# Two hybrid decoder layers in one core: the mean of each post-norm as two fp32r products of the sum's high and low part, placed one triple further on

## What is computed

```
def rmsnorm(x, g):
    xf = x.astype(jnp.float32)
    y = xf * lax.rsqrt(jnp.mean(xf * xf, axis=-1, keepdims=True) + RMS_EPS)
    return (y * g.astype(jnp.float32)).astype(x.dtype)
...
        x = x + rmsnorm(y, norm_post[i])
        gate = jax.nn.sigmoid(rmsnorm(x, pe_norm[i]) @ pe_w_gate[i])
        x = x + gate * (p[i] @ pe_w_proj[i])
```

## Time and profile before

| what | value |
| --- | --- |
| median of three executions | 636.34 us (635.78 to 637.64) |
| the profiled execution | 636.59 us |
| its span, first to last instruction | 634.5 us |
| granted TensorE clock, mean | 1.000 |
| PE busy | 625.3 us (99%) |
| weight loads on PE | 516.1 us (81%) |
| DVE busy | 393.7 us (62%) |
| ACT busy | 324.8 us (51%) |
| POOL busy | 297.5 us (47%) |

### The profile page before, as it was taken

One profiled execution on the slowest core, in us unless ns is written; L12 is line 12 of the kernel. 1 busy time (PEld: TensorE's weight loads), 2 busy tenths in 40 slices (PEclk: granted clock), 3 DMA queues, 4 the chain that ended last, 5 costly groups with the idle time before them and its releaser, 6 DMA issues.

```text
span 634.5 us, 9282 instructions
## 1 busy us (share of the span) xinstructions
PE 625.3 (99%) x2924; PEld 516.1 (81%) x2924; DVE 393.7 (62%) x787; ACT 324.8 (51%) x562; POOL 297.5 (47%) x400
## 2 busy tenths in 40 slices
PE   8999999999999999999999999999999999999997
PEld 6778888888888887888788888888888888887886
DVE  5678778787868687555969635342424243357874
ACT  7757666565757575565667633331222222556451
POOL 2785473645555455100347457546554742002470
PEclk9999999999999999999999999999999999999999
DMA  5443333433345333144003323323223332352031
GB/s 207 134 144 109 123 127 116 110 111 118 121 129 112 110 110 114 34 165 167 34 5 114 115 67 119 115 97 120 79 93 105 99 132 67 125 174 67 1 132 67
DMA packets 26585, 68.03 MB, mean 107 GB/s; under 512 B 3504, under 2 KB 9648, under 8 KB 26560
## 3 DMA queue, kind: packets, MB, share of 16 engines
q1 hardware_dynamic: 26560, 67.71, 32.5%
HBM read 65.57 MB, written 2.13 MB: 107 GB/s over the span
## 4 chain that ended last, share of the span: by engine, by line
PE 91%; ACT 3%; DVE 2%; DMA 1%; issue 1%; POOL 1%; SPq 0%; DVEq 0%; ACTq 0%
PE ps_pj L1104 25%; PE ps_pj L1106 25%; PE ps_pj L1105 25%; PE ps_tr L1113 3%; PE ps_o L1235 2%; PE ps_o L1234 2%; PE ps_tr L1104 1%; PE ps_tr L1106 1%; PE ps_tr L1105 1%; DMA w_raw<-in_weights 1%; PE ps_sc L1204 1%; PE ps_sc L1202 1%; ACT w_hi L484 1%; POOL w_lo L422 1%; PE ps_pj L1134 1%
## 5 line engine op out<-in xcount | busy, mean ns | idle before, releaser
L422 POOL TENSOR_TENSOR w_lo<-w_raw,w_hi 128x256 fp32r<-128x256 f32 x316 | 241.4, 797 | 133.2 <-ACT w_hi L484 125.3
L1104 PE MATMUL ps_pj<-act_hi,w_hi 128*128 128x512 f32 (+1 forms) x712 | 281.1, 395 | 0.2
L1106 PE MATMUL ps_pj<-act_hi,w_lo 128*128 128x512 f32 (+1 forms) x712 | 276.3, 388 | 0.0
L1105 PE MATMUL ps_pj<-act_lo,w_hi 128*128 128x512 f32 (+1 forms) x712 | 276.0, 388 | 0.0
L1106 PEld LDWEIGHTS ps_pj<-act_hi,w_lo 128*128 128x128 f32 x712 | 133.7, 188 | 28.0
L1104 PEld LDWEIGHTS ps_pj<-act_hi,w_hi 128*128 128x128 f32 x712 | 133.9, 188 | 25.5 <-issue 1.4
L1105 PEld LDWEIGHTS ps_pj<-act_lo,w_hi 128*128 128x128 f32 x712 | 134.0, 188 | 23.8
L484 ACT CAST w_hi<-w_raw 128x1024 fp32r<-128x1024 f32 x95 | 99.4, 1049 | 88.4 <-DMA w_raw<-in_weights 65.8
L461 POOL TENSOR_TENSOR acc<-acc,sq 128x512 f32<-128x512 f32 x14 | 22.5, 1605 | 115.4 <-ACT sq L650 115.1
L430 POOL TENSOR_TENSOR bias<-bias,mask 128x128 f32<-128x128 f32 x60 | 31.9, 563 | 70.0 <-DMA bias<-negc_scratch 70.0
L554 ACT ACTIVATE logit<-logit,nmax 128x128 f32<-128x128 f32 (+1 forms) x64 | 36.0, 563 | 45.7 <-DVE nmax L817 45.4
(11 more groups left out here) (156 smaller groups left out, 777.4 us busy)
## 6 DMA issues: line engine op xcount, KB each, us to landing
w_raw<-in_weights SPq DMA_DIRECT2D x100, 512.0 KB, 3.3
bias<-negc_scratch SPq DMA_DIRECT2D x15, 256.0 KB, 7.2
bias<-negc_scratch SPq DMA_DIRECT2D x15, 192.0 KB, 6.1
xT<-in_xT SPq DMA_DIRECT2D x8, 256.0 KB, 4.6
bias<-negc_scratch SPq DMA_DIRECT2D x15, 128.0 KB, 4.8
out<-xT SPq DMA_DIRECT2D x7, 256.0 KB, 2.8
p_in<-in_pT SPq DMA_DIRECT2D x2, 512.0 KB, 4.3
bias<-negc_scratch SPq DMA_DIRECT2D x15, 64.0 KB, 3.5
```

The lines of the kernel that those rows point to most:

```text
L422: last = nc.gpsimd.tensor_tensor(w_lo[place % RING][:, tiles], w_raw[stream(place) % RAW][:, tiles], w_hi[place % RING][:, tiles], ALU.sub ...
L1104: nc.tensor.matmul(out, w_h, a[0][:, k, tokens], start=k == first, stop=False)
L1105: nc.tensor.matmul(out, w_h, a[1][:, k, tokens], start=False, stop=False)
L1106: end = nc.tensor.matmul(out, w_l, a[0][:, k, tokens], start=False, stop=k == last)
```

## The change

Both post-norms use `split_mean` in place of `norm_mean`, which is gone. Its place is in front of the first triple of embedding tile 6 (`NORM_AFTER = KT - 2`, k == 0), which is one triple behind where `norm_mean` stood. ACT gets `acc_round` between scaling the last tile of y and rounding the weight slot, DVE gets `acc_rest` between adding the last square and that slot's low part. The calls of the other three norms get new numbers, since the counts of two semaphores now go up five times and not three.

```
-NORM_AFTER = KT - 3
+NORM_AFTER = KT - 2
...
                         act.wait_ge(p_loaded, 16 * l + 16)
                         nc.scalar.copy(p_hi[:], p_in[:]).then_inc(p_hi_done, 1)
+                acc_round(3 * l + 1)
                 weight_hi(SLOT_GATE[l] + 3, SLOT_GATE[l] + 3)
                 norm_scale(3 * l + 1, ps_o[:])
...
                         nc.vector.tensor_tensor(p_lo[:], p_in[:], p_hi[:], ALU.subtract).then_inc(p_ready, 1)
+                acc_rest(3 * l + 1)
                 slot_lo(SLOT_GATE[l] + 3)
                 dve.wait_ge(rs_ready, 3 * l + 2)
...
-                acc_rest(2 * l + 1)
+                acc_rest(3 * l + 2)
...
-            def norm_mean(n):
-
-                pe.wait_ge(acc_done, KT * n)
-                nc.tensor.matmul(ps_o[:], mean_f[:], acc[:], start=True, stop=True).then_inc(ms_done, 1)
...
                     for k in range(PLE_KT):
-                        if m == NORM_AFTER and k == 1:
-                            norm_mean(3 * l + 1)
+                        if m == NORM_AFTER and k == 0:
+                            split_mean(3 * l + 1)
                         end = products(bank, 0, (p_hi, p_lo), [k], 0, PLE_KT - 1, w)
...
-                split_mean(2 * l + 1)
+                split_mean(3 * l + 2)
```

More of the change, by code:

```diff
@@ L1047, in _ @@
                     continue
-                acc_rest(2)
+                acc_rest(3)
                 nc.vector.memset(cv_w[:, 0:TAPS - 1], 0.0).then_inc(cv_pad, 1)
@@ L1322, in _ @@
                     side_by_side(STEP_CONV, SLOT_CONV, act1, ACT_H[1],
-                                 between={KT - 3: lambda: split_mean(2)}, lead=True)
+                                 between={KT - 3: lambda: split_mean(3)}, lead=True)
                     def conv_steps(m, js):
```

## The result

The changed kernel takes 640.63 us (median of 6 executions, 639.25 to 641.49) against 636.25 us for the kernel before in the same comparison (635.62 to 637.64). The ratio is 1.0060, with a 95% interval of 1.0047 to 1.0074: 4.4 us slower, outside the forecast range of 636.5 to 639.0 us, and on the side to which I gave 0.12.

What follows compares the result with a forecast made beforehand. PE bounds the kernel but runs on the mean's chain at the gate's second tile, so a mean 0.67 us later costs 2 x 0.67 = 1.34 us on the 636.34 us median: 637.7 us, range 636.5 to 639.0.

Steps and rivals of the forecast that it cites:

- the side to which I gave 0.12: Whole kernel: slower by over 0.3%, chance 0.12, made of 0.07 for the collision and 0.05 for a slow measurement.
- PE runs on the chain's time at the gate's second tile: At 312.1 us PE waits for the chain from the mean; PE's savings vanish there, a later mean shows in full.
- The "issue": PE's 0.52 us idle before the gate's second tile, without a named releaser; claimed to be ACT's copy of embedding tile 3.
- The waits forecast at embedding tiles 2 and 3: Sign at embedding tiles 2 and 3: PE would wait there for copies that come 0.67 us later.
- PE's own price, 0.86 against 0.46 us: PE at each post-norm: fp32 mean 0.86 us, two fp32r products 0.46, saving 0.40 per place, 0.80 in both.
- The mean comes 0.67 us later: Chain at the post-norm: rounding, subtracting and a 0.22 us release put Ln at 303.05 us, where it stood at 302.38.
- PE idle 0.38 us at the new place, its saving gone at once: PE ahead of the split mean: ready at 302.01, let go at 302.39 us, so the 0.40 saving is lost waiting.
- Everything behind it to the copy of tile 3 is DVE and ACT work in a fixed order, started by Exp, and moves by 0.67: From the mean to ACT's copy of embedding tile 3: the whole stretch shifts rigidly by 0.67 us per post-norm.
- one collision more between DVE and POOL: Ahead of the copy of tile 3: one more long act_lo, 1.05 us per place, 639.8 us in all; chance 0.07.
- the sign named for it: Ahead of the copy of tile 3: one more act_lo of over 1.2 us would show the forecast wrong.
- The sum without it: Both post-norms: PE 0.67 us later at each, 2 x 0.67 = 1.34 us, giving 637.7 us.
- the bounds of the release: DVE's release of PE at the split mean: 0.10 to 0.35 us, so 0.55 to 0.80 per place, 637.4 to 637.9.

Runs made afterwards that it cites:

- the kernels without the meeting: Changed kernel with POOL's first addition held until DVE finishes x of tile 3, cut in two, or additions cut to one column: 637.37, 637.48, 637.32 us.
- the ten kernels above in which POOL isn't held: The kernel before, the changed kernel and their variants, except the two where POOL's first addition waits for x of tile 3; medians 636.25 to 640.63 us.
- POOL held in the kernel before: The kernel before with POOL's first addition for the gate norm held until DVE has finished x of tile 3: 637.27 us.

## Why the prediction was wrong

- *PE runs on the chain's time at the gate's second tile.* Right. The "issue" was the copy's release: with the change the same load comes 0.12 us behind the copy's end (313.66 + 0.56 = 314.22, then 314.34), as before. The waits forecast at embedding tiles 2 and 3 came too (0.31 and 0.76 us at their weight loads in layer 0).
- *PE's own price, 0.86 against 0.46 us.* Right in size, and worth nothing, as said. With the change the two products take from 302.66 to 303.12.
- *The mean comes 0.67 us later.* Right: 0.68. The release by DVE, for which I borrowed 0.22 us from a copy's, took that: acc_lo ends at 302.44, and the second product's row, at 302.89, puts the first one's real start at 302.66.
- *PE idle 0.38 us at the new place, its saving gone at once.* Right: 0.39, since it was ready at 302.27. The row of tile 6 starts 3.39 us behind the square (303.12 - 299.73), where it was 3.40.
- *"Everything behind it to the copy of tile 3 is DVE and ACT work in a fixed order, started by Exp, and moves by 0.67."* **This step failed.** One instruction in that stretch, ACT's copy of tile 0, was started by PE and not by the chain, and moved by 0.56 only. POOL's first addition, behind it, moved by 0.53 and DVE's act_lo by 0.69, so they changed places. That cost 1.31 us per place on top of the 0.68. The trace had the rows that tell it, ACT starting 0.04 us behind PE's end of the tile and 0.76 behind its own act_hi, and I had looked at the copies of tiles 1 and 3 only.
- *The rival "one collision more between DVE and POOL".* This is what happened, on an act_lo ahead of the copy of tile 3, and the sign named for it, an act_lo of over 1.2 us there, is the row of 1.77. It is one more ahead of that copy, not one more in all. I gave it 0.07 because "POOL is set off by ACT's squares of the new x, and these move with DVE's work". They move by 0.16 us less, and the lead was 0.09. I had priced the collision at 1.05 per place. It is 1.03 on act_lo (1.77 against 0.74) and 0.28 more on the addition to x of tile 3 (1.35 against 1.07), which before met the end of POOL's first addition and now meets the second. 2 x 0.68 + 2 x 1.31 = 3.98, what is seen.
- *The sum without it*, 1.34 us, is what the kernels without the meeting show, 1.3.

The range was built from the bounds of the release and a scatter. It left out a case whose condition, a lead of 0.09 us against a shift of 0.67, I had not worked out.

## What to carry to other kernels

Before a delay is called rigid, go through every instruction behind it on each engine and ask what released it: one that was released by the side that doesn't move will shift by less. Where DVE and POOL both read SBUF and start within some tenths of a microsecond of each other, the order of their starts is a term of the sum, priced at the rest of the first one's instruction. That is an upper bound by a little: act_lo was held for 1.03 us where POOL's row had 1.23 left, POOL for 0.52 where act_lo had 0.65 left. Write down the lead and compare it with the shift. Such a loss can be mended by an order alone: here one wait, or one instruction more on POOL per place, gave back 2.7 of 4.0 us.

No arrangement tried beats the kernel before by what can be measured. What could be gained is small, by an estimate from the rows: PE idles some 0.4 us per place there and could save 0.40 by the split products, 1.6 us in all.

## What the runs showed of the hardware

DVE and POOL hold each other up where both read two tiles from SBUF, and both ways. POOL's one-column addition takes 0.20 us when it starts 0.07 ahead of DVE's act_lo and 0.70 when it starts 0.09 behind it (the first additions of the changed kernel and of the kernel before, both cut to one column; rows of two kernels):

```profile
309.59 0.20 POOL L461 TENSOR_TENSOR acc<-acc,sq 128x1 f32<-128x1 f32 x1 [51.50 <-ACT sq L650]
309.66 0.75 DVE L987 SCALAR_TENSOR_TENSOR act_lo<-xT,g_pe,act_hi 128x512 fp32r<-128x512 f32 x1
```

```profile
307.41 0.75 DVE L985 SCALAR_TENSOR_TENSOR act_lo<-xT,g_pe,act_hi 128x512 fp32r<-128x512 f32 x1
307.50 0.70 POOL L461 TENSOR_TENSOR acc<-acc,sq 128x1 f32<-128x1 f32 x1 [50.97 <-ACT sq L650]
```

The waiting isn't shown as idle time in front of the instruction but inside its row, so nothing in the waits shows it, and a mean over the sixteen act_lo, which even fell with the change, hides it. DVE's products with the PSUM bank, one SBUF input each, took 674 to 689 ns in all sixteen cases before, also beside POOL:

```profile
L990 DVE TENSOR_TENSOR t_a<-yT,ps_o x16: 674/678/689, 303.6 to 594.9; 128x512 f32<-128x512 f32 x16
L981 DVE TENSOR_TENSOR xT<-xT,t_a x16: 691/693/1347, 304.4 to 595.7; 128x512 f32<-128x512 f32 x16
```

The Trainium skill, "SBUF — State Buffer", section "SBUF: two separate sides", says of an instruction with two SBUF inputs on DVE against one of POOL that reads SBUF: "whichever [...] starts first gets the pair for the whole instruction; the other fully blocks". The trace agrees on who goes first: of POOL's first addition and act_lo of tile 1, in the ten kernels above in which POOL isn't held and in both layers, the row that started first wasn't stretched, down to a lead of 0.04 us. The other one waits for a little less than the rest of that row, 0.13 to 0.20 us less. So behind a POOL row of 0.20 or 0.23 us that is 0.06 or 0.07 ahead, act_lo shows no wait: 0.75 us.

The 87 executions of the kernel before in the three sets took 634.72 to 640.15 us. Two executions were compared ahead of the post-norm, where their programs are the same: the kernel before and the fp32 mean one triple later. A window of both (core 0: window, busy time of PE, PEld, DVE, ACT, POOL, granted clock, DMA), each with the row that ends PE's first long wait:

```profile
8.05 0.41 PE L1152 MATMUL ps_sc<-act_hi,f_w 128*64 128x512 f32 x1 [0.84 <-DVE act_lo L765]
...
10.00:20.00 10.00, 10.00 (x44) 7.32 (x43) 7.66 (x12) 6.14 (x11) 5.62 (x8) 1.00 0.28 100
```

```profile
10.80 0.65 PE L1152 MATMUL ps_sc<-act_hi,f_w 128*64 128x512 f32 x1 [3.23 <-DVE act_lo L765]
...
10.00:20.00 10.00, 9.20 (x34) 6.53 (x35) 9.16 (x14) 8.42 (x14) 3.47 (x5) 0.83 0.20 78
```

In the second PE stood idle for 3.23 us first, up to 10.80, at a granted clock of 1.00. Then the clock was 0.50, the lower of its two levels, until about 14 us, with matmuls starting every 0.43 us where they start every 0.23 otherwise, and 1.00 again from 15. In the first 20 us 58 matmuls started in it and 77 in the other, and its last square of y came at 302.30 and not at 299.47. What makes that first act_lo late wasn't tried. This spread is why the gate distances, equal to 0.02 us between layers, tell these kernels apart better than their medians: POOL held in the kernel before has a median 0.8 us above that kernel's, not to be told from none, and the shorter distance.
